# Gather two experts' tokens first, transpose the modulation's sums, load it by halves, reorder the attention's copies, pipeline the norms, add h on TensorE

## What is computed

```python
for layer in range(2):
    m_lat = _modulation(silu(c), w_mod[layer], b_mod[layer])     # 1024 x 6144, split in six
    u_lat = h * (1 + m_lat[1]) + m_lat[0]
    y_lat = attention + pooling (layer 0) or short convolution (layer 1), with an output projection
    h = layer_norm(ALPHA * h + m_lat[2] * y_lat) * ln_mix_g + ln_mix_b
    f = _modulate(h, m_lat[3], m_lat[4])
    # router: softmax over 16 experts, each takes its 64 best tokens
    ye = (silu(xe @ w_g) * (xe @ w_u)) @ w_d * gate              # 16 experts, 1024 x 1024 each
    h = layer_norm(ALPHA * h + m_lat[5] * scatter_add(ye)) * ln_ffn_g + ln_ffn_b
```

## Time and profile before

| | us |
|---|---|
| median of 3 runs | 3255.61 |
| lowest, highest | 3248.65, 3257.32 |
| the profiled execution, its own time | 3256.57 |
| its span, first to last instruction | 3254.8 |

### The profile page before, as it was taken

One profiled execution on the slowest core, in us unless ns is written; L12 is line 12 of the kernel. 1 busy time (PEld: TensorE's weight loads), 2 busy tenths in 40 slices (PEclk: granted clock), 3 DMA queues, 4 the chain that ended last, 5 costly groups with the idle time before them and its releaser, 6 DMA issues.

```text
span 3254.8 us, 31937 instructions
## 1 busy us (share of the span) xinstructions
PE 2835.5 (87%) x13512; PEld 1830.4 (56%) x13512; DVE 1123.0 (35%) x1546; ACT 746.1 (23%) x1114; POOL 130.7 (4%) x120
## 2 busy tenths in 40 slices
PE   6977879888849979988885997999979999989997
PEld 4634444323328644423334764888769865468886
DVE  4344331111153351211125533333331488233233
ACT  2233210100021130100013412222221265132121
POOL 1210200000010020000001000000010000000000
PEclk8988989999969979999997998999987899989998
DMA  7852169999932138999991212232240300113321
GB/s 275 294 197 56 34 276 428 427 428 428 427 135 78 66 129 339 428 428 428 426 391 57 78 52 71 85 107 74 98 127 3 78 1 1 38 67 102 105 85 39
DMA packets 122254, 600.99 MB, mean 185 GB/s; under 512 B 7184, under 2 KB 12560, under 8 KB 96256
## 3 DMA queue, kind: packets, MB, share of 16 engines
q1 hardware_dynamic: 117056, 584.27, 45.5%
q0 software_dynamic: 5056, 14.69, 1.5%
HBM read 596.84 MB, written 2.10 MB: 184 GB/s over the span
## 4 chain that ended last, share of the span: by engine, by line
PE 67%; DMA 15%; DVE 11%; ACT 5%; issue 1%; POOL 0%; DVEq 0%; ACTq 0%; POOLq 0%
PE psum L281 65%; ACT scratch L269 5%; DMA weight_ring<-in_w_exp_down 5%; DVE scratch L231 4%; DMA weight_ring<-in_w_exp_up 4%; DMA scratch<-in_w_exp_down 3%; DMA weight_ring<-in_w_exp_gate 3%; PE psum L296 2%; DVE scratch L3020 1%; DVE scratch L244 1%; DVE scratch L264 1%; DVE scratch L1288 1%; DVE scratch L237 1%; DMA weight_ring<-in_w_mod 1%; DVE scratch L239 1%
## 5 line engine op out<-in xcount | busy, mean ns | idle before, releaser
L281 PE MATMUL psum<-scratch,scratch 128*128 128x512 f32 (+14 forms) x9424 | 1924.0, 410 | 133.3 <-DVE scratch L231 64.1
L281 PEld LDWEIGHTS psum<-scratch,scratch 128*128 128x128 f32 (+4 forms) x9424 | 1406.2, 188 | 641.3 <-issue 295.2
L281 PE MATMUL psum<-weight_ring,scratch 128*64 128x512 f32 (+2 forms) x2752 | 714.3, 622 | 105.0 <-ACT scratch L269 35.6
L281 PEld LDWEIGHTS psum<-weight_ring,scratch 128*64 128x64 f32 (+2 forms) x2752 | 241.9, 146 | 527.2 <-issue 398.6
L231 DVE TENSOR_TENSOR scratch<-weight_ring,scratch 128x2048 fp32r<-128x2048 f32 (+2 forms) x110 | 241.9, 2199 | 552.2 <-ACT scratch L269 550.8
L269 ACT ACTIVATE scratch<-psum 128x512 f32<-128x512 f32 (+4 forms) x324 | 188.1, 580 | 820.3 <-PE psum L281 509.1
L269 ACT ACTIVATE scratch<-weight_ring 128x2048 fp32r<-128x2048 f32 (+2 forms) x110 | 202.9, 1844 | 614.2 <-PE psum L281 582.3
L296 PE MATMUL psum<-consts,scratch 128*128 128x128 f32 (+1 forms) x984 | 158.0, 306 | 126.6 <-DVE scratch L237 60.8
L231 DVE TENSOR_TENSOR scratch<-scratch,psum 128x512 f32<-128x512 f32 x92 | 63.3, 688 | 561.2 <-PE psum L281 559.7
L231 DVE TENSOR_TENSOR scratch<-scratch,scratch 128x512 fp32r<-128x512 f32 (+10 forms) x334 | 207.6, 622 | 80.0 <-ACT scratch L269 69.7
L296 PEld LDWEIGHTS psum<-consts,scratch 128*128 128x128 f32 (+1 forms) x984 | 124.9, 164 | 177.1 <-issue 97.0
(11 more groups left out here) (100 smaller groups left out, 606.7 us busy)
## 6 DMA issues: line engine op xcount, KB each, us to landing
weight_ring<-in_w_exp_gate SPq DMA_DIRECT2D x40, 2048.0 KB, 18.8
weight_ring<-in_w_exp_up SPq DMA_DIRECT2D x38, 2048.0 KB, 20.6
weight_ring<-in_w_exp_down SPq DMA_DIRECT2D x38, 2048.0 KB, 20.7
weight_ring<-in_ffn_w SPq DMA_DIRECT2D x28, 2048.0 KB, 7.8
scratch<-in_w_exp_up SPq DMA_DIRECT2D x26, 2048.0 KB, 20.6
scratch<-in_w_exp_down SPq DMA_DIRECT2D x26, 2048.0 KB, 18.1
weight_ring<-in_w_mod SPq DMA_DIRECT2D x24, 2048.0 KB, 8.7
scratch<-in_w_exp_gate SPq DMA_DIRECT2D x24, 2048.0 KB, 20.6
```

Source lines behind the costliest of these rows:

```text
L281: ins = T.eng.matmul(out, lhsT, rhs, start=start, stop=stop)
```

## The change

- The first modulation comes in column halves 0 and 2, then 1 and 3; after the first pair, half of the chunks are modulated and their kv products issued. The token inputs are loaded in two parts, the second behind the landing of half 2.
- `sums` makes four transposes; VectorE reduces over the four partial rows, then adds the bias. `sum_cols` goes.
- The attention's values and transposes share a ring of four banks. ACT makes its first copy of transposes ahead of exp, and copies the values a step earlier; VectorE makes its copy ahead of the normalise.
- `norm_dve` is cut in `stats`, `finish` and `gained`; VectorE runs stats(t), gained(t-1), finish(t). In the last tile h is added in two halves, one by POOL and one by VectorE. In `MixerOut` ACT normalises tile t ahead of splitting t-1.
- The tokens of experts 0 and 1 are gathered first (128 columns); the other six follow during experts 0 and 1, and the second gather is spread over e = 2 to 4.
- The hidden values are transposed ahead of the next down (`flip`); ACT's split of y follows the next flip.
- `PARTS` is (0,4), (4,7), (7,8); for the last part PE puts h in the bank by a product with the identity, for six jobs ahead of the last down; the norm reads PSUM, and `z` has four buffers.

```diff
-            mm(T, bank[:, 2 * n:2 * n + 2], self.part(i)[:, s], k.sum_cols, True, True, *names)
+            tr(T, k, bank[:, n * P:(n + 1) * P], self.part(i)[:, s], *names)
...
-        bank = k.psum.of((*self.key, "sum", i))
-        tt(V, self.m["cols"][:, 4 * i:4 * i + 4, :], bank[:, 0:8].rearrange("p (a b) -> p a b", b=2),
-           self.m["bias_cols"][:, 4 * i:4 * i + 4].unsqueeze(2).to_broadcast([P, 4, 2]), ALU.add,
-           ("free", *self.key, "sum", i))
+        bank = k.psum.of((*self.key, "sum", i)).rearrange("p (n g r) -> p n r g", n=4, g=4)
+        cols = self.m["cols"][:, 4 * i:4 * i + 4, :]
+        reduce(V, cols, bank[:, :, 0:2, :], ALU.add, ("free", *self.key, "sum", i))
+        tt(V, cols, cols, self.m["bias_cols"][:, 4 * i:4 * i + 4].unsqueeze(2).to_broadcast([P, 4, 2]), ALU.add)
...
+    def pair_pe(self, T, i):
+
+        for j in (i, i + 2):
+            self.products(T, j, self.BANKS)
+        for j in (i, i + 2):
             self.sums(T, j, self.SUMS)
...
+    def norms_dve(self, V, between=None):
+
+        for t in range(NT):
+            self.stats(V, t)
+            if t:
+                self.gained(V, t - 1)
+            self.finish(V, t)
+        if between:
+            between(V)
+        self.gained(V, NT - 1)
...
+    def gained(self, V, t):
+
+        k = self.k
         V.wait_ge(*k.at(self.key, "norm", t))
         if t == 0:
             V.wait_ge(*k.at("loaded", f"{self.key}_gain"))
-        tt(V, self.z[:, b, :], self.z[:, b, :], self.gain, ALU.mult, (self.key, "gained", t))
+        if t < NT - 1:
+            tt(V, self.z_of(t), self.z_of(t), self.gain, ALU.mult, (self.key, "gained", t))
+            return
+        for half in range(2):
+            n = slice(half * HALF, (half + 1) * HALF)
+            tt(V, self.z_of(t, half), self.z_of(t, half), self.gain[:, n], ALU.mult, *([] if half else [(self.key, "gained", t)]))
+        tt(V, k.h[:, t, n], self.z_of(t, 1), self.bias[:, n], ALU.add, (self.key, "h rest"))
...
+    def combine(self, V, t, half):
+
         job = (self.key, "out", t, half)
         V.wait_ge(*self.k.at("full", *job))
-        tt(V, zb, self.k.psum.of(job), self.k.h[:, t, half * HALF:(half + 1) * HALF], ALU.add, ("free", *job))
+        return self.k.psum.of(job)
+
+    def normal(self, A, t, scale, bias):
+        for half in range(2):
+            job = (self.key, "out", t, half)
+            names = [("free", *job)] + ([(self.key, "norm", t)] if half else [])
+            if t >= self.z.shape[1]:
+                A.wait_ge(*self.k.at(self.key, "h", t - self.z.shape[1]))
+            act(A, self.z_of(t, half), self.k.psum.of(job), ACT.Identity, *names, scale=scale, bias=bias)
...
+            self.norm.norm_act(A, t)
             if t:
                 self.next.split_act(A, t - 1)
-                for q in range(2):
+                for q in range(2 if t < NT - 1 else 1):
                     self.next.turned_out(A, t - 1, q)
-            self.norm.norm_act(A, t)
...
-            self.norm.norm_dve(V, t)
+        self.norm.norms_dve(V, lambda V: self.next.turned_out(V, NT - 2, 1))
...
-        for r in (0, 1):
-            f.load_rows(Y, r)
+        for j in (0, 2):
+            f.load_half(Y, j)
         self.kv_units.load(Y)
-        for r in (2, 3):
-            f.load_rows(Y, r)
+        for j in (1, 3):
+            f.load_half(Y, j)
         self.q_units.load(Y)
...
+        f.pair_pe(T, 0)
         run = k.psum.take(T, ("kv", "in"), self.KV, 3).rearrange("p b (t n) -> p (b t) n", t=2)
         for i in range(2):
+            if i:
+                f.pair_pe(T, 1)
...
-    SCORES, TURNED, VALUES = (0, 4), (4, 7), (7, 8)
+    SCORES, TURNED = (0, 4), (4, 8)
...
+        for n in range(last + 3):
+            if 2 <= n < last + 2:
+                self.turned(A, n - 2, 0, 0)
             if n < last:
                 b = n % self.BUFS
                 A.wait_ge(*k.at("max", n))
@@ -1263,18 +1296,17 @@
                     act(A, self.prob[:, b, i, :], self.score_view(n)[:, i, :], ACT.Exp,
                         *([("exp", n), ("free", "scores", n)] if i else []),
                         bias=self.neg[:, b, i:i + 1], scale=1.0, accum_out=self.sum[:, b, i:i + 1])
+            if self.last_of_group(n - 3):
+                g = self.steps[n - 3][0]
+                A.wait_ge(*k.at("full", "values", g))
+                act(A, self.m["catT"][:, g, :], k.psum.of(("values", g)), ACT.Copy, ("free", "values", g))
             if (g := self.pool_step(n - 1)) is not None:
                 A.wait_ge(*k.at("full", "p out", g))
                 act(A, self.m["catT"][:, 4 + g, :], k.psum.of(("p out", g)), ACT.Copy, ("free", "p out", g),
                     scale=self.p_scale[:, g:g + 1])
             if 2 <= n < last + 2:
-                self.turned(A, n - 2, 0, 0)
                 self.turned(A, n - 2, 1, 0)
             self.filler.step_act(A, n)
...
+            if n >= 2:
+                self.turned(V, n - 2, 0, 4)
             if 1 <= n <= last:
                 self.normalise(V, n - 1)
-            if n >= 2:
-                self.turned(V, n - 2, 0, 4)
...
-    PARTS = ((0, 4), (4, 6), (6, 8))
+    PARTS = ((0, 4), (4, 7), (7, 8))
+    AHEAD = 6
...
+            if e < 2:
+                yield from (("rest", c) for c in range(4 * e, 4 * e + 4))
+            if 2 <= e <= 4:
+                yield from (("gather", c) for c in range(3 * e - 6, min(3 * e - 3, NC)))
+            yield "flip", e
             if 9 <= e <= 12:
                 yield from (("back", (0, *j)) for j in jobs[2 * (e - 9):2 * (e - 8)])
-            if e in (13, 14):
-                yield from (("back", (1, *j)) for j in jobs[4 * (e - 13):4 * (e - 12)])
+            if e in (14, 15):
+                yield from (("back", (1, *j)) for j in jobs[4 * (e - 14):4 * (e - 13)])
+        yield from (("plus", j) for j in jobs[:self.AHEAD])
         yield "down", E - 1
         yield from (("back", (2, *j)) for j in jobs)
...
+            self.is_slot(V, 0, t, 0, 2)
+        for q in range(2):
+            self.first_dve(V, q)
+        for t in range(NT):
+            self.is_slot(V, 0, t, 2, E // 2)
+        for t in range(NT):
+            self.is_slot(V, 1, t, 0, E // 2)
...
+    def first_pe(self, T):
+
+        for q in range(2):
+            job = (self.key, "first", q)
+            bank = self.k.psum.take(T, job)
+            for i in range(4):
+                self.gather(T, bank[:, i * P:(i + 1) * P], 4 * q + i, 0, 0, 2, *([("full", *job)] if i == 3 else []))
+
+    def first_dve(self, V, q):
+        k = self.k
+        job = (self.key, "first", q)
+        V.wait_ge(*k.at("full", *job))
+        for i in range(4):
+            c = 4 * q + i
+            ts(V, self.xeT[:, c, 0:P], k.psum.of(job)[:, i * P:(i + 1) * P], self.scale[:, c:c + 1],
...
+    def rest_pe(self, T, c):
+        job = (self.key, "gather", 0, c)
+        bank = self.k.psum.take(T, job)
+        self.gather(T, bank[:, P:HALF], c, 0, 2, E // 2, ("full", *job))
...
+        for q in (range(2) if e == 0 else ()):
+            T.wait_ge(*k.at("free", key, "first", q))
+        for c in (range(NC) if e in (2, 8) else ()):
...
+    def flip_act(self, A, e):
+
         k, key = self.k, self.key
         A.wait_ge(*k.at("full", key, "hid", e))
         if e >= 2:
             A.wait_ge(*k.at("full", key, "down", e - 2))
         act(A, self.hidT[:, e % 2], k.psum.of((key, "hid", e)).rearrange("p (a b) -> p a b", a=4), ACT.Copy, ("free", key, "hid", e))
+        if e:
+            self.down_act(A, e - 1)
...
+        if last and 2 * t + half >= self.AHEAD:
+            self.plus_pe(T, (t, half))
+        bank = k.psum.of(name) if last else k.psum.take(T, name)
...
+    def plus_pe(self, T, job):
+
+        k = self.k
+        t, half = job
+        T.wait_ge(*k.at(self.end_key, "back", 1, t, half))
+        bank = k.psum.take(T, (self.end_key, "out", t, half))
+        mm(T, bank, k.ident, k.h[:, t, half * HALF:(half + 1) * HALF], True, False)
```

More of the change, by code:

```diff
@@ L1566, in act @@
         for what, e in self.order():
-            {"slots": self.slots_act, "up": self.up_act, "down": self.down_act, "gates": self.nothing,
-             "gather": self.nothing, "back": self.nothing}[what](A, e)
+            {"slots": self.slots_act, "up": self.up_act, "flip": self.flip_act}.get(what, self.nothing)(A, e)
+        self.down_act(A, E - 1)
         for t in range(NT):
```

203 lines of the change are left out of this document (91 added, 112 removed).

## The result

The changed kernel takes 3284.94 us (median of 4 runs, 3282.71 to 3288.23) against 3255.76 before: the ratio is 1.0095 (95% interval 1.0076 to 1.0113), 29 us slower. The profiled execution has a span of 3286.3 us. The forecast was 3239.5, with a range of 3206 to 3264.

What follows compares the result with a forecast made beforehand. Bounds by stage: TensorE in layer 0's q and pool projections, TensorE with idle gaps in attention and mixers, weights' DMA in the experts. Sum -11 - 7 - 33 + 2 x (18 + 6 - 7) = -17: 3239.5 us, range 3206 to 3264.

Steps and rivals of the forecast that it cites:

- The mechanism of the attention: Attention: four-bank ring and new copy order leave a plain step bounded by scores, maximum and exp, 5.4 us; gain 33 us.
- the three waits of the projections: Output projections: TensorE waits for h three times, 6.5, 4.7 and 4.7 us, as stats(t) precedes gained(t-1); net +18 a layer.
- the front: First modulation by column halves: second half at 45.3 to 54.9, q projection at 58.5 instead of 69.46; -11 us.
- the sums: Layer 0's q and pool projections: 28 transposes replace seven groups of four products on TensorE; -7 us (-5 to -7.5).
- the prediction's list: Attention: step-by-step times counted from 147.98, plain steps 5.7 us, others up to 13.9, putting the last maximum at 260.
- the stalls: Attention: six stalls, each followed by a slow product (+1.7) and scores (+0.8), move the last maximum to 275.
- The clock behind them: Output projections: after each wait the next 3 to 4 us may run at half clock, +1.5 to 2 each, +5.5.
- the new end: End of the output projections' last tile: ACT's new order and h added by halves give back 3 to 4 us.
- Gathering ahead: Experts' start: stream gains nothing, up 2 waits for VectorE's copies, 6 us with 4 reaching the stream; net +6 a layer.
- The last experts: Before the last down: one more back part (5.6 us) and six h additions (5.2 us), some 6 us not covered.
- The norm: Experts' tail: norms overlap ACT and POOL, VectorE 3.5 us a tile, h at 942.5 against 949.7; tail net -7 a layer.
- The low-clock rival: Attention: clock stays at 1.2 GHz, 10 us a step, gain 6 instead of 33, kernel 3266.5 us; chance 0.15.

## Why the prediction was wrong

**What held.** The mechanism of the attention, the three waits of the projections one by one, and the additions of h. The direction of the front and the sums held too, each some 2 to 4 us too large: the second half of the modulation ran from 49.11 to 57.86, not from 45.3 to 54.9.

**What came out in part by luck.** Two sums fit better than their terms.

- *Attention, -33 forecast, -30.5 measured.* The 16 maxima have 15 steps between them; the prediction's list has 14, so a plain step of 5.7 us is missing. With it the list comes to 117.9 us; 128.1 were measured (134.77 to 262.86), so the stalls cost some 10 us over the list, not the 15 of the forecast. The tail from the last maximum to the projection grew by 4.8 us (262.86 to 286.97, against 310.29 to 329.63), forecast 1.5, at a granted clock of 0.72 where it was 0.91.
- *Projections, +18 forecast, +17.1 and +17.4 measured.* The waits are 15.95 us for 15.9. The clock behind them was put at +5.5 and the new end at -3 to -4. With the order of before, but the new end, the stage takes 101.0 us where it took 102.2: the new end gives 1.2. Then 18.3 - 15.95 = 2.4 is left for the clock. The two errors cancel.

**The step that failed: the experts, forecast -1 a layer, measured +18.7 and +20.9.** Three terms of it were mis-sized. In layer 0 the timelines of before and after divide it like this:

| stretch, us | before | after | difference | forecast |
|---|---|---|---|---|
| first gather to the second piece of down 13 | 437.4 | 452.9 | +15.4 | +6 |
| to the last part of the way back | 49.2 | 58.2 | +9.0 | +6 |
| to the end of the norms | 31.4 | 25.7 | -5.7 | -13 |

1. *Gathering ahead, forecast +6, measured +15.4, of which 14.6 went with the gather made whole.* Both holes were named, but the first was given some 2 us (the fifth piece at 475 to 481 against 474.54) and the second 4 of its 6 us. The stream idles for as long as no piece is freed beyond what is on the way, and here it paid each hole in full, since it is the bound from there on: 6.6 us (449 to 455.6), and 7.7 in 480 to 500 (0.37 and 0.40 of 10 us each). "Nothing is gained in the stream" was right and stopped short of "and something is lost". The first gather itself was put at 9.7 us and took 15.2, so that up 0 came 17 us behind its start, not 12; the stream, held up by the fifth piece, shows nothing of it.
2. *The last experts, forecast 6 us until the split ends, measured 9.0.* I had put 6 us of new work ahead of the last down and left DMA as the bound there. With the parts cut at pair 7, TensorE has a wait of 3.3 us and 46.5 us without pause: it is the bound, and the 10 us by which the stream was ahead at down 13 (859.12 against 869.25 for its second piece) are spent by the end of the last down (913.3 against 914.4).
3. *The norm, forecast 3.5 us a tile, measured 5.8.* I added the engines' own times and forgot that VectorE and GpSimd hinder each other; the gain behind the last down is 5.7 us in place of 13. Yet the trace of before has a case: an operation of 512 columns, 0.69 us elsewhere, took 2.01 beside GpSimd's addition:

```profile
384.97 2.35 POOL L754 TENSOR_TENSOR h<-scratch,scratch 128x1024 f32<-128x1024 f32 x1 [11.35 <-DVE scratch L231]
...
385.86 2.01 DVE L244 SCALAR_TENSOR_TENSOR scratch<-h,scratch 128x512 f32<-128x512 f32 x1
```

The low-clock rival did not come: the attention rose to 0.88. The slow result came from a side for which there was no rival, only a range: the gather's ended at +11 and the tail's (last experts and norm) at -3, and they measured +15.4 and +3.3. With the experts at no change the kernel would have come to some 3248 (3255.6 - 43 + 35, an estimate from the table of stages), so the earlier terms alone left little of the gain.

## What to carry to other kernels

Where weights stream through a ring, ask of any work moved behind the first use: how long does the engine free no piece, and how much is on the way then; what exceeds it is lost in full. A pipeline of norms pays where nothing waits for the tile before; where the next matmul waited for it, as here, one tile after the other was faster. Don't price a matmul with few columns by its columns: take a row with the same operand standing still, read with the same step.

## What the runs showed of the hardware

- A product of the gather (a 128x128 fp32r operand standing still and read with a step of four elements, 128 columns moving) takes 0.22 to 0.24 us at a granted clock of 0.50 and of 0.88 alike; with 512 columns 0.23 to 0.25 at a full clock (35 in 8.00 us, 64 in 16.2). A kv product (read without a step, 256 columns) takes 0.12 at a full clock. The transposes, also 128 columns, took 0.13 to 0.15 at a full clock and 0.24 to 0.25 at 0.50 (12 in 2.82 us at 267.53, 8 in 1.98 at 324.56).
- The narrow products let the clock fall though TensorE had no pause: 0.86 to 0.88 in their first 5 us, 0.50 in 412 to 417. With the same 52 added products ahead of them, the wide ones stayed at 1.00 (386 to 396 us of that run).
- An operation of VectorE on 128x1 elements with two inputs in SBUF waited for GpSimd's addition to end (2.13 us instead of 0.16), while the reciprocal ahead of it, 20 ns behind GpSimd's start, took its 0.16, and in the run with the other order statistics that read PSUM ran beside GpSimd in their usual 1.50 (906.06, beside the addition at 906.04). The Trainium skill (SBUF — State Buffer, section "Who interferes with whom") states that an instruction of VectorE with two SBUF inputs contends with one of GpSimd that reads SBUF, over a pair of ports whose lock is exclusive; these rows agree, and the run with the other order got the 2 us back, since the small operation there no longer falls beside an addition.
